# One tile of the last gate unit moved between the values of the last two pairs of heads

## The reference

```python
def _forgetting_attention(q, k, v, log_f):
    c = lax.cumsum(log_f.astype(jnp.float32), axis=2)
    def block(args):
        qb, cb, i = args
        z = jnp.einsum('bhqd,bhkd->bhqk', qb, k).astype(jnp.float32) * scale
        z = z + cb[..., :, None] - c[..., None, :]
        mask = key_pos[None, :] <= q_pos[:, None]
        p = jax.nn.softmax(jnp.where(mask, z, neg), axis=-1)
        return jnp.einsum('bhqk,bhkd->bhqd', p.astype(v.dtype), v)
...
g_sb, g_fx, g_mem = jnp.split(jax.nn.sigmoid(u @ w_gate[l] + b_gate[l]), N_BRANCH, axis=-1)
merged = (g_sb * (_merge_heads(o_sb) @ w_br_sb[l])
          + g_fx * (_merge_heads(o_fx) @ w_br_fox[l])
          + g_mem * (_merge_heads(o_mem) @ w_br_mem[l]))
```

## Time and profile before

| | us |
|---|---|
| runs: median (lowest, highest) | 3142.64 (3137.49, 3145.12) |
| profiled execution, its own time | 3145.6 |
| span in the profile | 3143.8 |
| mean granted TensorE clock | 0.968 |
| PE busy | 2974.6 (95%) |
| PEld (weight loads of PE) busy | 2762.0 (88%) |
| DVE busy | 1718.4 (55%) |
| ACT busy | 1435.3 (46%) |

### The profile page before, as it was taken

The page is one execution under the profiler, slowest core; times in us unless marked ns, Lnnn a source line. Parts: engine busy times, 40 slices in busy tenths (PEclk is TensorE's granted clock), DMA queues, the critical chain, the costliest instruction groups (busy, mean ns, idle before and its releaser), DMA issues.

```text
span 3143.8 us, 53947 instructions
## 1 busy us (share of the span) xinstructions
PE 2974.6 (95%) x23720; PEld 2762.0 (88%) x23720; DVE 1718.4 (55%) x2029; ACT 1435.3 (46%) x1831; POOL 160.9 (5%) x197
## 2 busy tenths in 40 slices
PE   8998898999998898999999999999889999999998
PEld 8988898999988898998989899898879899886887
DVE  5464555545554555545555645545676454464555
ACT  4455655445455655444445444444451344344444
POOL 1000100000000100001000000000011000044000
PEclk9999999999999999999999999999889999898999
DMA  6553334554553334555554445454320155440453
GB/s 244 188 181 120 122 137 159 188 188 174 188 185 123 122 136 154 187 188 210 186 201 163 157 179 188 177 186 172 134 81 4 70 187 186 145 162 22 158 183 134
DMA packets 69395, 492.89 MB, mean 157 GB/s; under 512 B 7854, under 2 KB 9422, under 8 KB 10535
## 3 DMA queue, kind: packets, MB, share of 16 engines
q1 hardware_dynamic: 64224, 465.53, 41.2%
q10 hardware_dynamic: 4938, 23.92, 2.0%
HBM read 488.32 MB, written 1.06 MB: 156 GB/s over the span
## 4 chain that ended last, share of the span: by engine, by line
PE 80%; DVE 8%; ACT 6%; POOL 2%; issue 2%; PEld 1%; DMA 0%; PEldq 0%; ACTq 0%; DVEq 0%; POOLq 0%; SPq 0%
PE bank L105 52%; PE acc L105 28%; DVE weights_lo L313 2%; ACT weights_hi L118 2%; POOL conv_gate L3073 1%; POOL conv_out L3076 1%; DVE tmp L671 1%; DVE h L664 1%; DVE h L679 1%; PEld acc L105 0%; DVE b_x_lo L503 0%; PE acc L999 0%; DVE b_x_lo L731 0%; ACT L1067 0%; ACT L1133 0%
## 5 line engine op out<-in xcount | busy, mean ns | idle before, releaser
L313 DVE TENSOR_TENSOR weights_lo<-weight_ring,weights_hi 128x2048 fp32r<-128x2048 f32 x440 | 1009.6, 2295 | 944.8 <-ACT weights_hi L118 944.4
L105 PE MATMUL bank<-b_x_hi,weights_hi 128*128 128x256 f32 x3576 | 1015.8, 284 | 21.7 <-DVE b_x_lo L731 16.9
L105 PE MATMUL bank<-b_x_hi,weights_lo 128*128 128x256 f32 x3576 | 1011.1, 283 | 0.0
L118 ACT ACTIVATE weights_hi<-weight_ring 128x2048 fp32r<-128x2048 f32 x440 | 839.5, 1908 | 375.6 <-PE acc L105 364.7
L105 PE MATMUL bank<-b_x_lo,weights_hi 128*128 128x256 f32 x3576 | 1010.6, 283 | 0.0
L105 PEld LDWEIGHTS bank<-b_x_hi,weights_hi 128*128 128x128 f32 x3576 | 679.7, 190 | 34.3 <-issue 18.9
L105 PEld LDWEIGHTS bank<-b_x_lo,weights_hi 128*128 128x128 f32 x3576 | 680.0, 190 | 3.3
L105 PEld LDWEIGHTS bank<-b_x_hi,weights_lo 128*128 128x128 f32 x3576 | 679.1, 190 | 0.0
L105 PE MATMUL acc<-weights_hi,b_hidden_hi 128*128 128x512 f32 x832 | 329.5, 396 | 0.0
L105 PE MATMUL acc<-weights_hi,b_hidden_lo 128*128 128x512 f32 x832 | 328.2, 394 | 0.0
L105 PE MATMUL acc<-weights_lo,b_hidden_hi 128*128 128x512 f32 x832 | 327.5, 394 | 0.0
(11 more groups left out here) (487 smaller groups left out, 4029.7 us busy)
## 6 DMA issues: line engine op xcount, KB each, us to landing
weight_ring<-in_weights SPq DMA_DIRECT2D x440, 1024.0 KB, 4.8
xn<-in_norm_rows ACTq DMA_DIRECT2D x14, 1024.0 KB, 4.8
sgu_bias_row<-in_sgu_rows ACTq DMA_DIRECT2D x1, 2048.0 KB, 10.8
sgu_norm_rows<-in_sgu_rows ACTq DMA_DIRECT2D x1, 2048.0 KB, 9.7
bias_hankel<-bias_scratch ACTq DMA_DIRECT2D x1, 1536.0 KB, 7.0
h<-in_x SPq DMA_DIRECT2D x2, 512.0 KB, 6.6
mem_norm<-in_memory SPq DMA_DIRECT2D x1, 1024.0 KB, 13.8
sgu_w_spatial<-in_sgu_w_spatial ACTq DMA_DIRECT2D x1, 1024.0 KB, 4.8
```

Of the source, the lines that this page charges most:

```text
L105: return pe.matmul(out, a, b, start=start, stop=stop, skip_group_check=True)
L118: return act.activation(out, in_, ACT.Copy, scale=scale)
L313: dve.tensor_tensor(k.w.lo[:, n % 2, :], k.ring[:, n % RING, :], k.w.hi[:, n % 2, :], ALU.subtract) \
```

## The change

The branch `fox` gets a table of its own. Its first 14 steps are those of `FOUR`. In the last six, `gate_b` of the last unit no longer stands ahead of `values` 1 but ahead of `values` 3:

```diff
+FOUR_LATE = FOUR[:14] + (("turn", 2), ("values", 1), ("turn", 3), ("values", 2), ("gate_b", 3), ("values", 3))
...
-        for what, n in FOUR:
+        for what, n in (FOUR_LATE if name == "fox" else FOUR):
```

## The result

| | before | changed |
|---|---|---|
| median of 20 runs, us | 3140.1 (3133.12 to 3145.6) | 3145.32 (3138.89 to 3151.59) |
| profiled execution: span, us | 3143.8 | 3147.8 |
| mean granted TensorE clock | 0.968 | 0.967 |

The ratio is 1.0018, with a 95% interval of 1.0010 to 1.0027. The changed kernel is some 5 us slower; the interval is 3.1 to 8.5 us. The forecast was 5.0 us more, within the 0.3% that it called no change. The three runs of before that stood ahead of the forecast had a median of 3142.64; with 20 it is 3140.1.

The account below looks back on a forecast made before the run. TensorE was taken as the bound; 2.6 us for the longer stretch at two places plus 2.4 us for low clock made 5.0 us on a median of 3142.6, forecasting 3147.6 us, range 3139 to 3155.

Parts of the forecast that it names:

- TensorE's stream is the bound: Whole kernel: TensorE is busy 95% of the span and its own work is 80% of the chain of waits.
- The new wait: Ahead of `turn` 3, at two places: TensorE idles 2.67 us until DVE's copy has emptied bank 4.
- The two waits removed: Idle of 0.16 us ahead of `values` 2 and 0.96 ahead of `values` 3 goes, 1.12 us a place.
- The place: From start of `turn` 2 to the merge's first product: 12.44 us before, 13.7 after at full clock; two places give 2.6.
- some 0.3: Term subtracted at each place: some 0.3 us by which `turn` 3 and `values` 2 now overlap.
- Sigmoids, table load, weight unit, SP: ACT's moved gate work, the gate's later-freed weight unit and SP's load queue: all hidden, costing nothing; sigmoids 0.5 us to spare.
- The clock: Low clock behind the new idle: 1.6 us a stretch, one and a half stretches over two places, 2.4 us (0 to 3.2).
- rival C: From the follow-up runs: the clock after the new idle costs nothing, or a low stretch only replaces a later one; no chance given.
- The page on the clock gate: Skill rule that only idle gaps over about 3 us lose the clock; 2.67 us would be free, the sum 2.6.
- absorption: Rival: TensorE waits later for something that doesn't move, such as a weight load, absorbing the loss; 3142.6 us, chance 0.05.
- gain: Rival: no new wait ahead of `turn` 3, both old idle times go; 2.2 us less, 3140.4 us, chance 0.05.
- the slow tail: Rival: clock stays low through `gate_b`, `values` 3 and merge, 25 us at most, 3167; chance 0.10 including other unseen causes.

Follow-up runs that it names:

- the filled kernel: Changed kernel with 11 products that nobody reads filling the new idle ahead of `turn` 3 in both `fox` layers; ratios to before 1.0015 and 1.0014.
- the filled merges: Kernel before with 9 or 10 products that nobody reads ahead of each of the block's six merges; ratio to before 0.9999 (0.9988 to 1.0010).

## Why the prediction was right, and where it was off

- *TensorE's stream is the bound.* Right; the place grew and the time with it.
- *The new wait.* Right in kind, place and releaser, shown by the changed profile and by the two moves of DVE's low part. It was 2.46 us for 2.67. `values` 1 starts 0.75 us after the start of `turn` 2, where `gate_b` started 0.58 after it; the end of the wait is DVE's and stayed (4.72 us after `turn` 2, 4.76 forecast).
- *The two waits removed.* Right, 1.12 us a place.
- *The place.* 13.96 at full clock, 13.7 forecast: 1.53 more than before and not 1.29. The mis-sized term is the step from `turn` 3 to `values` 2, taken as 0.58 from a pair of steps in which products of the gate followed the transposes. With `values` behind them it is 0.80. In the prediction's sum by terms it is the "some 0.3" of overlap, which did not come: 2.46 less 1.12 is 1.34, and the place grew by 1.53. That adds 0.5 us for the two places, which makes 3.1 for 2.6.
- *Sigmoids, table load, weight unit, SP.* Right, free. ACT waited 0.60 us ahead of the last take, 0.5 forecast.
- *The clock.* Price right at 1.6 us a stretch, frequency too high: four of eight, not six. At the places it is 1.6 us for both and not 2.4. The sum with both terms as measured is 4.7 for 5.0: the two mis-sizings, 0.5 up and 0.8 down, nearly cancelled, and that the number came out so close is luck. How much of this part is in the time of the whole kernel isn't shown: the filled kernel, which lacks it, was timed 4.4 to 4.7 us above before, inside the interval of both views. That more low clock is there over the whole span is shown, by 0.9688 against 0.9701; rival C in the form "a low stretch only takes the place of another" doesn't fit the changed kernel. It does fit the filled merges, whose mean clock stayed at 0.9701 and whose time stayed too. Why the two edits differ stays open, and so does what a low stretch early in the program is worth at its end.
- *The page on the clock gate.* By the rule of the Trainium skill ("TensorE: Matmul & The Clock Gate", "Why this matters for your kernels") the new idle, under 3 us, would cost nothing. At the places the trace disagrees in four of eight. For the time of the kernel the runs decide neither way; its mean granted clock, 0.9688 against 0.9701, speaks against the rule too.
- *The rivals.* No absorption and no gain; the clock came back after one stretch each time, so the slow tail didn't come.

## What to carry to other kernels

Before a step is moved away from between a producer's stream and a shared buffer, look at what else its time covered: the margin here was 0.34 us between DVE's copy and `turn` 3, and 2.98 us of cover were taken from it to fill a wait of 0.96. When such a move looks right on one engine, move the other engine's large instruction with it, into the same new cover; neither half gains alone here. In a kernel whose untouched part scatters by 14 us between executions, judge an edit of 1 to 2 us by the length of its own stretch, and where the edit acts on the clock, by the mean granted clock of many executions too: the filled merges were 5.6 us faster in their own stretch and nothing in all.

## What the runs showed of the hardware that I had not expected

From the start of six transposes to the start of the next products it was 0.58 us where these were the gate's, and 0.74 to 0.81 where they were those of the values and didn't wait for bank 6; no run shows why. An idle time of TensorE of the same 2.46 us is followed by a low stretch in one execution and not in the next, at the same place of the same program. And taking the low stretch from four of six merges early in the program (5.6 us by the profile) showed neither in its time nor in the mean granted clock of 12 executions, while the new idle times of the changed kernel went with a mean lower by 0.0013.
